# First adaptive modulation of a two-block network in three portions of its weights, and the order of work around three row norms

## The chip, the cores and the metric

One NeuronCore of one Trainium2 chip runs the whole program. The metric is the device time of one launch in microseconds (us), median over several runs; lower is better. A profiled execution of the same program gives the trace.

## The reference

Batch 1, 256 tokens `x` and 256 context tokens `ctx`, width 1024. A first network has two layers of adaptive normalisation: a retention mixer, then differential attention, each followed by a feed-forward network (FFN) with a convolution. A second network mixes two kinds of attention and a recurrence and ends in a plain FFN. All weights are float32. What the change touches first is the opening of layer 0:

```python
def ada_mod(cvec, w, b):                       # w: 1024 x 6144
    m = jax.nn.silu(cvec) @ w + b
    return jnp.split(m[:, None, :], 6, axis=-1)
shm, scm, gm, shf, scf, gf = ada_mod(c, ada_w[l], ada_b[l])
ux = modulate(rms_norm(h_x, norm_g[l, 0]), shm, scm)      # xn * (1 + scale) + shift
uc = modulate(rms_norm(h_c, norm_g[l, 0]), cshm, cscm)    # the same with c_ctx's vectors
p = u @ w_in                                              # first retention product, 1024 x 8192
```

Shift `shm` and scale `scm` are columns 0 to 2047 of `ada_w[0]` (8 MB). Feature f of 128 columns (f = 0 to 7) of the modulated rows needs only its own 128 columns of shift and of scale.

## The kernel before, in words

Every large product is done as three float32r products of high and low halves (`three`, L586). Weights come in steps of four units of 128 x 1024 (512 KB), one in each of four slots `raw[:, j]`. SyncE issues their loads in one fixed order (L465 to L571). For each unit ScalarE copies the high half to `wh` (L1548) and VectorE subtracts to get the low half `wl` (L2310); both functions are called `split`. TensorE then multiplies the unit (96 matmuls of 512 columns in a step of the retention input). A slot is reloaded once `lo_done` says that its low half is there. The order of work on each engine is written out by hand and semaphores join the engines; PSUM is used as two halves of four banks, `main` and `side`.

**The opening.** GpSimd issues the loads of the identity, the picks, the tokens (`load_residual`, L3344: 1 MB `x` into `res[:, 0:2]`, 1 MB `ctx` into `res[:, 2:4]`), then a dozen small vectors (`load_rows`, L3335), the bias table, and after `lo_done` reaches 2 (L3393) the two retention decays, the retention constants `kret` (1.1 MB) and a ring of later modulation weights (`load_mods`). SyncE loads columns 0 to 2047 of `ada_w[0]` in four chunks of 512 columns through the four `raw` slots (L502 to L508), a slot being loaded again when TensorE has used it (`ada_used`), and only then the first retention weights (`load`, L465). For chunk n TensorE multiplies the four units by the two condition vectors (`first_ada`, L744, matmuls at L633), ScalarE copies the result out (`keep_ada`, L1571), TensorE turns it (`turn_ada`, L637) and VectorE adds the bias (`take_ada`, L2351). ScalarE squares the token rows and takes roots (`row_square`, L1579), VectorE scales them (`normalise_row`, L2392), TensorE transposes two tiles of 128 tokens at a time into PSUM (`turn_part`, L731). When all four chunks are in, VectorE forms `1 + scale` times the gain (`scales`, L2403), and ScalarE (`apply_even`, L1587) and VectorE (`apply_part`, L2424) modulate feature by feature straight out of PSUM and write high and low halves `uh` and `ul`. The first retention step (L888) goes over its four units for tokens 0 to 255, takes the second pair of token tiles in between, and goes over the units again for the context. VectorE then computes the logarithm of the decays' sigmoid (`log_sigmoid`, L2490), and both engines wait for the constants before they split the second step's units (L1699, L1700, L2529).

**The three norms.** After differential attention (L1283), after the second FFN (L1293) and after the second network's mixer (L1520), 256 rows are normalised in two tiles. ScalarE takes the mean square of the product in PSUM (`rms`, L1617), VectorE scales and adds it to the residual (`finish_rows`, L2722), ScalarE squares the new residual (`norm_rows`, L1631), VectorE takes the reciprocal (L2453) and scales tile 0 (L2457), ScalarE scales tile 1 (L1639). In the second part ScalarE splits all four units of the next step (`split()`, L1870, L2259) before it waits for the new residual. TensorE transposes the tiles (`turn_normed`, L688) and fills its waits with matmuls of the identity (`keep_clock`, L720: 16 and 10 calls, two instructions each); `prep` (L1643, L2461) then modulates and forms halves, after which the next product starts. After the mixer there is no scaling between; VectorE adds the product to the residual (`add_plain`, L3272).

Of the kernel before, what the change touches and what calls it, by code (L numbers as in the profile page):

```python
# [8 lines left out]
ALU = mybir.AluOpType  # L9
# [174 lines left out]
def build(nc, a, out):  # L184
    ctx = ExitStack()
    with ctx:
# [76 lines left out]
        norm_a = (area(0, KD, SEQ), [area(8 + 4 * t, D) for t in range(4)])  # L263
# [107 lines left out]
        raw_loaded = [sem(f"raw_loaded{j}") for j in range(SLOTS)]  # L371
        hi_done = sem("hi_done")
# [32 lines left out]
        xn_act, xn_vec = sem("xn_act"), sem("xn_vec")  # L405
# [55 lines left out]
        def _(sp):  # L461
# [3 lines left out]
            def load(parts):  # L465

                s = S.next()
                for j in range(SLOTS):

                    if isinstance(s, int) and s == 0:  # L470
                        sp.wait_ge(ada_used, 12 + j + 1)
                    else:
                        sp.wait_ge(lo_done, s * SLOTS + (j - SLOTS + 1))
                    pieces = parts(j)
                    for dst, src in pieces:
                        sp.dma_start(dst, src).then_inc(raw_loaded[j], 32 // len(pieces))
# [33 lines left out]
            kq, kk, kv = RH * RDK, 2 * RH * RDK, RH * RDV  # L510
            for h in range(RH):
                load(pair(w, h * RDK, h * RDK + kq))
# [62 lines left out]
        def _(pe):  # L575
# [98 lines left out]
            def turn_rows(batch, n, loads):  # L674

                pe.wait_ge(rows_loaded[batch], 16 * loads)
                begin_row()
                pe.transpose(ps[:, main, 0:n], rows[0:n, batch, :], ident[0:n, 0:n]).then_inc(turned, 1)

            def begin_row():  # L680


                if G.next():
                    pe.wait_ge(emptied, G.now() - 1)
# [3 lines left out]
            def turn_normed(nt):  # L688
# [13 lines left out]
                for part in range(2):  # L702
                    for t in tiles_of(nt, part):
                        v, x = (vec_turned, act_turned)[t % 2], (xn_vec, xn_act)[t % 2]
                        v[0] += 1
                        pe.wait_ge(x, v[0])
# [11 lines left out]
            vec_turned, act_turned = [0], [0]  # L718
# [25 lines left out]
            def first_ada(n):  # L744

                if n > 1:
                    pe.wait_ge(ada_kept, n - 1)
                for u in range(SLOTS):
                    if (n, u) == (1, 2):
                        turn_part(0, norm_a[1][0:2], side)  # L750
                    pe.wait_ge(raw_loaded[u], 32 * (n + 1))
                    ada_matmuls(n, u, raw[:, u, :], main + 3 - n % 2)

            def first_turn(n):
# [3 lines left out]
                turn_ada(n, main + 1)  # L758

            first_ada(0)  # L760
            turn_rows(2, 96, 2)
            first_turn(0)
            first_ada(1)
            turn_rows(1, 113, 9)
            first_turn(1)
            first_ada(2)
            turn_rows(3, 88, 2)
            turn_rows(4, 88, 2)
            pe.wait_ge(hot_loaded, 32)
            pe.wait_ge(tab_set, 1)  # L770
            begin_row()
            pe.matmul(ps[0:16, main, 0:384], tab, hot, start=True, stop=True).then_inc(turned, 1)
            first_turn(2)
            first_ada(3)
            first_turn(3)

            def dense_tokens(half, passes=((0, 1, 2, 3),), fresh=0):
# [4 lines left out]
                for x, tiles in enumerate(passes):  # L782
                    for j in range(SLOTS):
                        pe.wait_ge(lo_done, base + j + 1)
                        if fresh:
                            pe.wait_ge(part_low, SLOTS * (fresh + x - 1) + j + 1)
                        for k in range(2):
                            f = 2 * j + k
                            for t in tiles:
                                mm = three(ps[:, half + t, :], uh[:, f, t * P:(t + 1) * P], ul[:, f, t * P:(t + 1) * P],  # L790
                                           wh[:, j, k * 512:(k + 1) * 512], wl[:, j, k * 512:(k + 1) * 512], f == 0, f == KD - 1)
                        if x == len(passes) - 1:
                            mm.then_inc(unit_used, 1)
                        yield SLOTS * x + j
# [87 lines left out]
            for h in range(RH):  # L882
                d = 4 * h
                dense = G.now()
                if h == 0:
                    pe.wait_ge(ada_kept, 4)
                    pe.wait_ge(ada_taken, 4)
                    for j in dense_tokens(main, ((0, 1), (2, 3)), fresh=1):  # L888
# [2569 lines left out]
```

## Time and profile before

| what | value |
|---|---|
| median of 3 runs | 1867.37 us (1866.85 to 1868.1) |
| the profiled execution, its own time | 1869.95 us |
| its span, first to last instruction | 1868.2 us |
| what lies around the span | 1.75 us |
| TensorE busy | 96% of the span |
| VectorE, ScalarE, GpSimd busy | 61%, 45%, 5% |
| mean granted TensorE clock | 0.986 of full speed |
| mean DMA rate | 151 GB/s |

TensorE's clock has two levels, 2.4 GHz (1.00) and 1.2 GHz (0.50). A busy share says how long instructions of an engine were in flight; adjacent matmuls overlap, so the distance between two starts is what one costs. Idle time matters only on the engine that everything else waits for.

### The profile page before, as it was taken

What the parts mean: (1) busy time and instruction counts of PE and PEld (TensorE: products, weight loads), DVE (VectorE), ACT (ScalarE), POOL (GpSimd) and SP (SyncE); (2) the same over time, 40 slices, a digit from 0 to 9 for tenths busy, and PEclk for the clock granted to TensorE, in tenths of its full rate; (3) what the DMA queues carried; (4) which work ended last, traced back from release to release, by engine and by line L of the source; (5) the groups of instructions that cost most, each with busy time, mean ns of one, the idle gap of its engine ahead of it and who ended that gap; (6) DMA issues with size and microseconds to landing.
All of it is one profiled execution on the core that took longest, in us unless ns stands there. A gap on an engine that the chain in (4) does not pass through costs nothing. (4 is left out here: it accounts for less than half of the span.)

```text
span 1868.2 us, 26242 instructions
## 1 busy us (share of the span) xinstructions
PE 1795.1 (96%) x9865; PEld 1499.7 (80%) x9865; DVE 1143.2 (61%) x1525; ACT 837.2 (45%) x1213; POOL 86.9 (5%) x164
## 2 busy tenths in 40 slices
PE   5999999999999999999998998899999999989997
PEld 2877777777678888888887887899879987879985
DVE  2766757667358678644347556566665695855554
ACT  3333233232456432233335556566554546544553
POOL 2011001100000010000000000000001000000000
PEclk8999999999999999999999999999999999999999
DMA  8654444545255376432323222455545554546562
GB/s 289 196 156 144 151 146 151 164 144 151 94 214 180 124 227 188 146 94 79 113 69 112 80 79 83 141 181 181 190 148 184 162 158 146 181 139 187 180 193 100
DMA packets 150909, 282.38 MB, mean 151 GB/s; under 512 B 12651, under 2 KB 78307, under 8 KB 150688
## 3 DMA queue, kind: packets, MB, share of 16 engines
q1 hardware_dynamic: 133344, 220.54, 36.9%
q0 software_dynamic: 17472, 60.57, 10.5%
q8 instruction: 63, 1.03, 0.2%
q14 instruction: 30, 0.25, 0.0%
HBM read 276.83 MB, written 4.23 MB: 150 GB/s over the span
## 5 line engine op out<-in xcount | busy, mean ns | idle before, releaser
L2310 DVE TENSOR_TENSOR wl<-raw,wh 128x1024 fp32r<-128x1024 f32 (+1 forms) x388 | 454.6, 1181 | 383.7 <-ACT wh L1548 381.3
L1548 ACT ACTIVATE wh<-raw 128x1024 fp32r<-128x1024 f32 (+1 forms) x388 | 393.5, 1022 | 617.5 <-PE ps L590 605.0
L588 PE MATMUL ps<-uh,wh 128*128 128x256 f32 (+1 forms) x1216 | 381.9, 314 | 7.8 <-DVE spare L2332 7.8
L589 PE MATMUL ps<-ul,wh 128*128 128x256 f32 (+1 forms) x1216 | 379.8, 312 | 0.0
L590 PE MATMUL ps<-uh,wl 128*128 128x256 f32 (+1 forms) x1216 | 379.6, 312 | 0.0
L588 PE MATMUL ps<-wh,uh 128*128 128x512 f32 (+2 forms) x960 | 367.4, 383 | 9.7 <-issue 6.2
L589 PE MATMUL ps<-wl,uh 128*128 128x512 f32 (+2 forms) x960 | 354.1, 369 | 0.0
L590 PE MATMUL ps<-wh,ul 128*128 128x512 f32 (+2 forms) x960 | 353.8, 369 | 0.0
L588 PEld LDWEIGHTS ps<-uh,wh 128*128 128x128 f32 x1216 | 233.9, 192 | 22.9 <-issue 7.0
L590 PEld LDWEIGHTS ps<-uh,wl 128*128 128x128 f32 x1216 | 233.8, 192 | 12.7
L589 PEld LDWEIGHTS ps<-ul,wh 128*128 128x128 f32 x1216 | 233.9, 192 | 12.3
L588 PE MATMUL ps<-wh,ah 128*128 128x512 f32 x584 | 229.3, 393 | 0.9 <-DVE al L2444 0.7
L590 PE MATMUL ps<-wh,al 128*128 128x512 f32 x584 | 227.4, 389 | 0.0
L589 PE MATMUL ps<-wl,ah 128*128 128x512 f32 x584 | 227.3, 389 | 0.0
L588 PEld LDWEIGHTS ps<-wh,uh 128*128 128x128 f32 x960 | 182.3, 190 | 52.8 <-issue 23.0
L589 PEld LDWEIGHTS ps<-wl,uh 128*128 128x128 f32 x960 | 182.4, 190 | 33.6 <-issue 5.3
L590 PEld LDWEIGHTS ps<-wh,ul 128*128 128x128 f32 x960 | 182.2, 190 | 30.7
L2371 DVE SCALAR_TENSOR_TENSOR arena<-arena,cvec 128x1024 f32<-128x1024 f32 x140 | 173.7, 1281 | 8.8 <-DMA arena<-in_ada_w 0.8
L588 PEld LDWEIGHTS ps<-wh,ah 128*128 128x128 f32 x584 | 109.6, 188 | 26.1 <-issue 3.4
L590 PEld LDWEIGHTS ps<-wh,al 128*128 128x128 f32 x584 | 109.6, 188 | 23.1
L589 PEld LDWEIGHTS ps<-wl,ah 128*128 128x128 f32 x584 | 109.7, 188 | 22.8 <-issue 0.5
L860 PE MATMUL ps<-res,arena 128*128 128x512 f32 x160 | 72.5, 600 | 3.0 <-DVE res L2607 2.1
(305 smaller groups left out, 1490.5 us busy)
## 6 DMA issues: line engine op xcount, KB each, us to landing
raw<-in_ffn_w_up SPq DMA_DIRECT2D x176, 256.0 KB
arena<-in_ada_w POOLq DMA_DIRECT2D x80, 512.0 KB, 4.1
raw<-in_w_in SPq DMA_DIRECT2D x60, 512.0 KB
raw<-in_ret_w_in SPq DMA_DIRECT2D x48, 512.0 KB
raw<-in_ffn_w_down SPq DMA_DIRECT2D x40, 512.0 KB
raw<-in_ret_w_out SPq DMA_DIRECT2D x32, 512.0 KB
raw<-in_w_up SPq DMA_DIRECT2D x32, 512.0 KB
raw<-in_w_down SPq DMA_DIRECT2D x32, 512.0 KB
```

The costliest lines, as they stand in the source:

```text
L588: pe.matmul(o, lh, rh, start=first, stop=False)
L589: pe.matmul(o, lh, rl, start=False, stop=False)
L590: return pe.matmul(o, ll, rh, start=False, stop=last)
L860: mm = pe.matmul(ps[:, half + t % 2, :], v0[:, c:c + P], vres[:, k, :], start=n == 0, stop=n == len(reads[t]) - 1)
L1548: T.mark(act.activation(wh[:, j, 0:size], raw[:, j, 0:size], ACT.Copy), hi_done)
L2310: T.mark(vec.tensor_tensor(wl[:, j, 0:size], raw[:, j, 0:size], wh[:, j, 0:size], ALU.subtract), lo_done)
L2371: ins = vec.scalar_tensor_tensor(out=o, in0=w, scalar=c32[:, k, c:c + 1], in1=o, op0=ALU.mult, op1=ALU.add)
```

## The change

1. **Portions.** The four chunks become: n = 0, columns 0 to 511 (shift of f = 0 to 3); n = 1, columns 1024 to 1535 (scale of f = 0 to 3); n = 2, shift and scale of f = 4, 5; n = 3, of f = 6, 7. Chunks 2 and 3 are loaded as two DMAs of 256 KB per unit (rows of 1 KB). So the first portion is chunks 0 and 1, the second chunk 2, the third chunk 3. Eight areas `first` of the arena hold them in place of the `raw` slots, so the first retention units can be loaded in between: units 0 and 1 after chunk 1, unit 2 after chunk 2, unit 3 after chunk 3.
2. **Tokens on SyncE's queue.** `x` and `ctx` are loaded by two DMAs of SyncE ahead of all weights. The later reload of the same two stays with GpSimd.
3. **Opening compute.** All four token tiles are transposed early; ScalarE and VectorE copy them to `xt` in SBUF and modulate from there (`apply_first`: on VectorE two scalings, the split of unit j, two subtractions). TensorE runs `keep_clock` with 20 calls, then multiplies the first retention step in one pass (`dense_first`, which waits before unit j for `lo_done` j + 1 and `part_low` 2j + 2), with chunks 2 and 3 and the small transposes between its eighths.
4. **Decays.** Their two small DMAs are issued before the wait, and `log_sigmoid` comes after the first portion. The constants' load waits for `ada_used` 16 in place of `lo_done` 2.
5. **Norms.** VectorE scales both tiles; ScalarE no longer waits for the reciprocal except for the one before; its splits go one unit per part (two after the mixer), the rest after the squares; VectorE's last two splits move into `prep`; `keep_clock` has 12 and 6 calls in place of 16 and 10.

```diff
+        rows_a, xt = [area(8 + 4 * t, D) for t in range(4)], area(24, KD, TOK)
+        first = [area(kb, UNIT) for kb in (0, 4, 40, 44, 54, 58, 71, 75)]
@@ sync
-            for c in range(4):
-                part = cols(a["ada_w"][0], c * 512)
-                for j in range(SLOTS):
-                    if c:
-                        sp.wait_ge(ada_used, 4 * (c - 1) + j + 1)
-                    for dst, src in part(j):
-                        sp.dma_start(dst, src).then_inc(raw_loaded[j], 32)
+            sp.dma_start(res[:, 0:2, :], a["x"][0].rearrange("(t p) n -> p t n", p=P)).then_inc(rows_in[0], 16)
+            sp.dma_start(res[:, 2:4, :], a["ctx"][0].rearrange("(t p) n -> p t n", p=P)).then_inc(rows_in[1], 16)
+            def load_first(n, u):
+                i = 4 * n + u
+                if i >= 8:
+                    sp.wait_ge(ada_used, i - 7)
...
+            for n in range(4):
+                for u in range(SLOTS):
+                    load_first(n, u)
+                for j in ((), (0, 1), (2,), (3,))[n]:
+                    load_unit(part, j)
@@ tensor
+            for u in range(2):
+                first_ada(0, u)
+            turn_part(0, rows_a[0:2], main)
+            for u in range(2, SLOTS):
+                first_ada(0, u)
+            pe.wait_ge(xt_act, 1)
+            pe.wait_ge(xt_vec, 1)
+            turn_part(2, rows_a[2:4], main)
             turn_rows(2, 96, 2)
+            for u in range(2):
+                first_ada(1, u)
+            turn_rows(1, 113, 9)
             first_turn(0)
+            for u in range(2, SLOTS):
+                first_ada(1, u)
             first_turn(1)
+            pe.wait_ge(xt_act, 2)
+            pe.wait_ge(xt_vec, 2)
+            keep_clock(ps[:, side + 3, 384:TOK], 20)
+            for j, k in dense_first(main):
+                if (j, k) in ((0, 0), (1, 0)):
+                    for u in range(SLOTS):
+                        first_ada(2 + j, u)
+                elif (j, k) in ((0, 1), (1, 1)):
+                    first_turn(2 + j)
+                    turn_rows(3 + j, 88, 2)
+                elif (j, k) == (2, 0):
+                    turn_table()
@@ turn_normed
-                                keep_clock(ps[:, halves[0] + 3, 384:TOK], 16)
+                                keep_clock(ps[:, halves[0] + 3, 384:TOK], 12)
-                        keep_clock(ps[:, halves[0] + 3, 384:TOK], 10)
+                        keep_clock(ps[:, halves[0] + 3, 384:TOK], 6)
@@ scalar, opening
+            def apply_first(j):
+                f = 2 * j
+                T.settle()
+                for k in range(2):
+                    x = xt[:, f, k * SEQ:(k + 1) * SEQ]
+                    T.mark(act.activation(x, x, ACT.Identity, scale=acol[:, k, f:f + 1], bias=mcols(k, f, 1)), act_own)
+                T.settle()
+                for k in range(2):
+                    act.wait_ge(part_odd, 2 * j + k + 1)
+                    T.mark(act.activation(uh[:, f:f + 2, k * SEQ:(k + 1) * SEQ], xt[:, f:f + 2, k * SEQ:(k + 1) * SEQ], ACT.Copy), part_hi)
+            squares(0)
+            squares(1)
+            keep_xt(0)
+            keep_ada(0, side + 3)
+            keep_xt(1)
+            keep_ada(1, side + 2)
+            split(units=range(0, 1))
+            act.wait_ge(acol_ready, norms[0])
+            apply_first(0)
+            split(units=range(1, 2))
+            apply_first(1)
             act.wait_ge(z_abs, 1)
             T.mark(act.activation(lgt[:, 2, :], lgt[:, 1, :], ACT.Exp, scale=-1.0), lg_exp)
+            for n in (2, 3):
+                keep_ada(n, side + 5 - n)
+                split(units=range(n, n + 1))
+                act.wait_ge(acol_ready, norms[0])
+                apply_first(n)
@@ scalar, norm_rows and finish_rows
+                if rms_parts[0] > 1:
+                    act.wait_ge(rstd_ready, rms_parts[0] - 1)
                 T.mark(rms(tiles, lambda t: res[:, t, :], D, (0, 4)), rms_done)
-                act.wait_ge(rstd_ready, rms_parts[0])
-                for t in tiles:
-                    if t % 2:
-                        T.mark(act.activation(xn[:, t, :], res[:, t, :], ACT.Copy, scale=st[:, 8 + t:9 + t]), xn_act)
...
-                    if part:
-                        split()
+                    split(units=range(part, part + 1))
                     wait_residual(part)
                     norm_rows(nt, part)
+                split(units=range(2, SLOTS))
@@ scalar, after the mixer
-                if part:
-                    split()
                 wait_residual(part)
                 norm_rows(2, part)
+                split(units=range(2 * part, 2 * part + 2))
@@ vector, opening
+            for t in range(3):
+                normalise_row(t, t, rows_a[t])
+            keep_xt(0)
+            normalise_row(3, 3, rows_a[3])
+            keep_xt(1)
             take_cols(bcol[:, :], 96)
             take_cols(gcol[:, 0:113], 113)
+            take_ada(0, side + 1)
+            take_ada(1, side + 1)
+            first_scales(0, 4)
+            apply_first(0)
+            apply_first(1)
+            log_sigmoid()
+            take_ada(2, side + 1)
+            first_scales(4, 6)
+            apply_first(2)
             take_cols(fcol2[:, :], 88)
             take_cols(fcol[:, 16:104], 88)
+            take_ada(3, side + 1)
+            first_scales(6, 8)
+            apply_first(3)
@@ vector, norm_rows and prep
-                    if t % 2 == 0:
-                        T.mark(vec.tensor_scalar(xn[:, t, :], res[:, t, :], st[:, 8 + t:9 + t], None, ALU.mult), xn_vec)
+                    T.mark(vec.tensor_scalar(xn[:, t, :], res[:, t, :], st[:, 8 + t:9 + t], None, ALU.mult), xn_vec)
...
+                    if half:
+                        split(units=range(2, 3))
                     hb = group_full()
...
+                split(units=range(3, 4))
@@ vector, finish_rows
-                    norm_rows(nt, part, range(2) if part else ())
-                split(units=range(2, SLOTS))
+                    norm_rows(nt, t, range(t, t + 1))
@@ gpsimd
-            load_residual()
...
+            for z, name in enumerate(("ret_decay_f", "ret_decay_b")):
+                pool.dma_start(lgt[:, 0, 4 * z:4 * z + 4], a[name].to_broadcast([P, RH])).then_inc(decay_loaded, 16)
...
-            pool.wait_ge(lo_done, 2)
-            for z, name in enumerate(("ret_decay_f", "ret_decay_b")):
-                pool.dma_start(lgt[:, 0, 4 * z:4 * z + 4], a[name].to_broadcast([P, RH])).then_inc(decay_loaded, 16)
+            pool.wait_ge(ada_used, 16)
```

## Rows read from the trace of the kernel before

**Rows 1.** the page, busy time of the engines over the whole span

```profile
PE 1795.1 (96%) x9865; PEld 1499.7 (80%) x9865; DVE 1143.2 (61%) x1525; ACT 837.2 (45%) x1213; POOL 86.9 (5%) x164
```

**Rows 2.** who TensorE waited for: total us, times, longest

```profile
PE ps L588 <- DVE spare L2332: 7.8, 3, 2.8
...
PE ps L699 <- DVE arena L2457: 5.6, 2, 4.2
```

**Rows 3.** stretches: length, busy time, TensorE clock, DMA share, GB/s

```profile
20.00:22.00 2.00, 2.00 (x15) 1.50 (x8) 0.00 (x0) 0.00 (x0) 0.00 (x0) 1.00 1.01 371
...
42.00:44.00 2.00, 0.12 (x1) 0.15 (x1) 1.97 (x3) 1.83 (x4) 0.00 (x0) 0.50 0.97 340
...
48.00:50.00 2.00, 2.00 (x7) 1.58 (x6) 1.97 (x3) 0.58 (x1) 0.83 (x2) 0.54 0.91 101
```

**Rows 4.** timeline of the opening: start us, us, engine, line, operation

```profile
12.26 1.06 ACT L1582 ACTIVATE junk<-res 128x1024 bf16<-128x1024 f32 x1 [6.39 <-DMA res<-in_x]
...
20.50 2.93 PE L737 MATMUL ps<-ident,arena 128*128 128x128 f32 x16
...
25.54 1.07 PE L633 MATMUL ps<-raw,cvec 128*32 128x256 f32 x16
...
39.38 0.98 PE L642 MATMUL ps<-pick,adas 128*128 128x4 f32 x4 [0.60 <-ACT adas L1577]
...
40.88 0.99 DVE L2415 TENSOR_SCALAR arena<-ps,acol,mcol 128x256 f32<-128x256 f32 x2
...
41.52 0.63 ACT L1598 ACTIVATE uh<-arena 128x512 fp32r<-128x512 f32 x1
...
41.80 1.21 DVE L2310 TENSOR_TENSOR wl<-raw,wh 128x1024 fp32r<-128x1024 f32 x1
...
43.04 0.69 DVE L2422 TENSOR_TENSOR ul<-arena,uh 128x512 fp32r<-128x512 f32 x1
...
43.88 0.77 PE L588 MATMUL ps<-wh,uh 128*128 128x512 f32 x1 [3.52 <-DVE ul L2422]
...
54.92 1.91 PE L737 MATMUL ps<-ident,arena 128*128 128x128 f32 x16
...
64.21 1.41 DVE L2504 SCALAR_TENSOR_TENSOR lgt<-lgt 128x12 f32<-128x12 f32 x7
...
70.54 1.03 ACT L1759 ACTIVATE arena<-ps 128x1024 f32<-128x1024 f32 x1 [1.27 <-PE ps L590]
```

**Rows 5.** DMA issues: size of one, us from issue to landing

```profile
arena<-in_k_ret POOLq DMA_DIRECT2D x1, 1152.0 KB, 8.7
```

**Rows 6.** timeline, first changed norm (after the second attention)

```profile
1186.10 5.37 PE L724 MATMUL ps<-ident 128*128 128x128 f32 x32
...
1187.72 1.23 DVE L2739 TENSOR_TENSOR res<-res,arena 128x1024 f32<-128x1024 f32 x1
...
1190.05 1.06 ACT L1624 ACTIVATE junk<-res 128x1024 bf16<-128x1024 f32 x1
...
1191.74 2.40 PE L724 MATMUL ps<-ident 128*128 128x128 f32 x20
...
1191.76 1.15 ACT L1639 ACTIVATE arena<-res,st 128x1024 f32<-128x1024 f32 x1 [0.23 <-DVE st L2453]
...
1193.97 1.04 PE L699 MATMUL ps<-ident,arena 128*128 128x128 f32 x8
...
1197.46 0.36 PE L588 MATMUL ps<-uh,wh 128*128 128x256 f32 x1 [2.45 <-DVE spare L2332]
```

**Rows 7.** timeline, second changed norm (after the second FFN)

```profile
1397.13 0.39 PE L588 MATMUL ps<-uh,wh 128*128 128x256 f32 x1 [2.57 <-DVE spare L2332]
```

**Rows 8.** timeline, third changed norm (after the mixer)

```profile
1663.75 1.22 DVE L3283 TENSOR_TENSOR res<-res,ps 128x1024 f32<-128x1024 f32 x1 [1.68 <-PE ps L590]
...
1667.79 1.06 ACT L1624 ACTIVATE junk<-res 128x1024 bf16<-128x1024 f32 x1
...
1674.56 0.55 PE L588 MATMUL ps<-uh,wh 128*128 128x256 f32 x1 [2.76 <-DVE spare L2332]
```

More of the change, by code:

```diff
@@ L371, in build @@
         raw_loaded = [sem(f"raw_loaded{j}") for j in range(SLOTS)]
+        first_loaded = [sem(f"first_loaded{j}") for j in range(8)]
+        xt_act, xt_vec = sem("xt_act"), sem("xt_vec")
+        rows_in = (sem("x_in"), sem("ctx_in"))
         hi_done = sem("hi_done")
@@ L468, in load, with load_unit @@
                 for j in range(SLOTS):
[L470 to L476, printed above, removed]
+                    sp.wait_ge(lo_done, s * SLOTS + (j - SLOTS + 1))
+                    load_unit(parts, j)
+            def load_unit(parts, j):
+                pieces = parts(j)
+                for dst, src in pieces:
+                    sp.dma_start(dst, src).then_inc(raw_loaded[j], 32 // len(pieces))
             def cols(w, c0, n=512):
@@ L677, in turn_rows @@
                 begin_row()
-                pe.transpose(ps[:, main, 0:n], rows[0:n, batch, :], ident[0:n, 0:n]).then_inc(turned, 1)
+                pe.transpose(ps[:, side, 0:n], rows[0:n, batch, :], ident[0:n, 0:n]).then_inc(turned, 1)
+            row_groups = Count()
             def begin_row():
-                if G.next():
-                    pe.wait_ge(emptied, G.now() - 1)
+                G.next()
+                if row_groups.next():
+                    pe.wait_ge(emptied, row_groups.now() - 1)
             turned_norms = [0]
@@ L757, in first_turn, with turn_table, dense_first @@
                     pe.wait_ge(ada_taken, n)
-                turn_ada(n, main + 1)
-            first_ada(0)
+                turn_ada(n, side + 1)
+            def turn_table():
+                pe.wait_ge(hot_loaded, 32)
+                pe.wait_ge(tab_set, 1)
+                begin_row()
+                pe.matmul(ps[0:16, side, 0:384], tab, hot, start=True, stop=True).then_inc(turned, 1)
+            def dense_first(half):
+                G.next()
+                S.next()
+                for j in range(SLOTS):
+                    pe.wait_ge(lo_done, j + 1)
+                    pe.wait_ge(part_low, 2 * j + 2)
+                    for k in range(2):
+                        f = 2 * j + k
+                        for t in range(4):
+                            mm = three(ps[:, half + t, :], uh[:, f, t * P:(t + 1) * P], ul[:, f, t * P:(t + 1) * P],
+                                       wh[:, j, k * 512:(k + 1) * 512], wl[:, j, k * 512:(k + 1) * 512], f == 0, f == KD - 1)
+                        if k:
+                            mm.then_inc(unit_used, 1)
+                        yield j, k
@@ L765, in _ @@
             first_turn(1)
[L766 to L777, printed above, removed]
+            pe.wait_ge(xt_act, 2)
@@ new lines, in apply_first @@
+            def apply_first(j):
+                f = 2 * j
+                for k in range(2):
+                    x = xt[:, f + 1, k * SEQ:(k + 1) * SEQ]
+                    T.mark(vec.tensor_scalar(x, x, acol[:, k, f + 1:f + 2], mcols(k, f + 1, 1), ALU.mult, ALU.add), part_odd)
+                split(units=range(j, j + 1))
+                T.settle()
+                for k in range(2):
+                    vec.wait_ge(part_hi, 2 * j + k + 1)
+                    o = slice(k * SEQ, (k + 1) * SEQ)
+                    T.mark(vec.tensor_tensor(ul[:, f:f + 2, o], xt[:, f:f + 2, o], uh[:, f:f + 2, o], ALU.subtract), part_low)
@@ L2520, in _ @@
             tick(emptied)
-            take_ada(2, main + 1)
-            for t in range(2, 4):
-                normalise_row(t, t, norm_a[1][t])
-            take_ada(3, main + 1)
-            scales(0, 8)
-            apply_part(0, side, norm_a[0], 0, 0, lambda j: split(units=range(j, j + 1)))
-            apply_part(1, side, norm_a[0], 1, 0)
-            log_sigmoid()
             vec.wait_ge(const_loaded, 16)
@@ L3292, in _ @@
                 norm_rows(2, part, range(2) if part else ())
-            split(units=range(2, SLOTS))
             prep(2, MLPG0, None)
```

151 lines of the change are left out of this document (74 added, 77 removed).

## The prediction

> **What bounds the kernel now.** First the page: TensorE has something in flight for 96% of the span, 1795.1 us, VectorE 61%, ScalarE 45% [rows 1]. So time is won only where TensorE waits or works at half rate. Then who it waited for: three times 2.6 us on average for the first half of a modulated norm, twice for normalised rows [rows 2]. The largest loss is the opening. In the timeline the first product that counts, a matmul of the retention step, starts at 43.88 us, released by the first feature's low half [rows 4]; what TensorE does before is small (condition vectors, transposes). From there it is not idle until long after, so whatever moves 43.88 forward moves the end, provided later inputs keep up. ScalarE's read of the first step's result at 70.54 marks where that step ends [rows 4].
>
> The clock needs care. The stretch from 20 to 22 us is printed with 1.00, yet 16 transposes started at 20.50 took 2.93 us, and the same 16 at 54.92 took 1.91 [rows 3, 4]; so part of the early work ran at 1.2 GHz although the column says otherwise. In 42 to 44 it is 0.50, and in 48 to 50 it is 0.54, which puts the rise at about 49.8 (0.5 and 1.00 weighted by time) [rows 3]. The step therefore spent 6.0 us at half rate, worth 3.0, then 70.4 - 49.8 - 1.9 for the transposes = 18.7: 21.7 us at full rate, 2.7 for an eighth of it.
>
> **Part 1, when the first portion is there.** Bytes move at 371 GB/s with rows of 2 KB or more, and at 340 with rows of 1 KB, both at full DMA share [rows 3]. Before the end of chunk 1 come 2.1 MB of tokens, 4.2 MB of chunks 0 and 1, and some 0.3 MB of small loads: 6.6 MB / 0.371 = 17.8 us, after about 3.3 us until the first bytes: 21.1. The tokens have to come anyway; ahead of the weights they delay chunk 0, and the squares can start near 7.5 instead of 12.26 [rows 4]. Each 512 KB unit of 1 KB rows then takes 1.54: units 0 and 1 by 24.2, chunk 2 by 30.4, unit 2 by 31.9, chunk 3 by 38.1, unit 3 by 39.6. SyncE's waits (`ada_used`, then `lo_done`) are all met by then. I count the 16 half-size DMAs and their issue at nothing beyond that rate, since the queue is ahead of the engines; if it weren't, the price is the second rival's.
>
> **Part 2, TensorE until the first product.** Chunk 0's first two units at about 12 to 14, the first transposes (16, up to 3.6 us if all at half rate, twice the 1.91 of full rate less overlap), chunk 0's rest to 19.5, the second transposes some 2.5 to 22. Then, at full rate: a turned bias 0.4, two units 1.07 (25.54 in [rows 4]), a wait of 0.3 for VectorE's copies, gains 0.4, turn 0.6, two units 1.07 to 25.9, ScalarE's copy 0.4, the second turn 0.6 to 27.0. That is 6 us behind the data, since the order on TensorE puts all four tiles first. VectorE adds and scales by 27.5. Then the 40 instructions of `keep_clock`: 20 took 2.40 us at full rate [rows 6], so 4.7, to 31.7.
>
> **Part 3, the first feature pair.** Unknown is modulation out of SBUF; from PSUM two of VectorE took 0.99, at 40.88 in [rows 4]. Nothing excludes a gain: between 0.4 and 1.0 for two. I take 0.8. Then VectorE's split 1.21 and two subtractions of 0.69 [rows 4]: with gaps 3.6 us. ScalarE's two modulations and two copies of 0.63 fit beside it. 27.5 + 3.6 = 31.1, so `keep_clock` covers this chain: the first product starts at 31.7, against 43.88. Between ends: 27.5 if the turns hurry and `keep_clock` does not bind, 36.4 if all of its 40 run at half rate (another 4.7).
>
> **Part 4, the first step with its guests.** Eight eighths 21.7; chunks 2 and 3, 32 instructions each at full rate, 2.1 each (two units 1.07) = 4.3; two turns (0.98 at half rate, 39.38 in [rows 4]) 1.2; three small transposes 1.7; waits between them 0.4: 29.3 us, to 61.0. The order waits for nobody: chunk 2 is there at 30.4 and wanted at 34.4; chunk 3 is there at 38.1 and wanted at 43. Unit 1's features are low at 34.5, wanted at 40. `log_sigmoid` (seven steps 1.41, some 4 in all [rows 4]) now stands on VectorE before `take_ada` 2: 34.5 to 38.6, while TensorE turns chunk 2 at 39.5, so it is covered by 1 us, and without cover costs at most 4 once. The third portion is turned at 48.5, plus 4.5 for scales and features = 53, wanted at 55. So the first step ends at 61.0 instead of 70.4: **9.4 us**. The transposes (1.9) that stood inside the step are in Part 2.
>
> The decays' DMAs are earlier and cost GpSimd two issues in a stretch in which nobody waits for it: nothing. The constants are issued at about 45 and land 8.7 later [rows 5], 54; a split on ScalarE (1.06) and VectorE (1.21) makes unit 0 of step 2 at 56.5, wanted at 61.
>
> **Part 5, the three norms.** In the first, ScalarE spent 3.9 us on four splits, so the squares of tile 1 came at 1190.05 though the residual was added at 1188.95; ScalarE's scaling ended at 1192.9, and TensorE, held by its own fillers (5.37 + 2.40), transposed at 1193.97 [rows 6]. Now: squares at 1189.0, root at 1190.5, VectorE's scaling (at most the 1.15 of ScalarE's, I take 0.8) ends 1191.5 instead of 1192.9. Fillers: 24 and 12 instructions in place of 32 and 20. Part of the first batch is at half rate (32 in 5.37 are 15 slow and 17 fast, at 0.23 and 0.117), so 24 are 4.5 and 12 are 1.4: transposes at 1192.4. Gain 1.6. ScalarE's last two splits end at 1192.7, in time; the split that VectorE now does between the halves (1.2) delays only units 2 and 3, which TensorE wants 5.8 us after it starts. The second has the same order, and there the last splits on ScalarE bind by 1.6 as well: its product would start near 1395.5 instead of 1397.13 [rows 7]. In the third the residual was ready at 1664.97 and the squares came at 1667.79, 2.8 late [rows 8]. Now squares at 1665.0, but VectorE does two splits (2.4) before the reciprocal, scaling done 1668.3, fillers (2.8 + 0.5 + 1.4 at full rate) until 1668.7, product at 1671.7 for 1674.56: 2.9. Together **6.1**. Between ends: 3 if the shorter fillers bring half-rate spells (each about 1.7, three of them would take 5.1; one is there already at the third), 8 if a spell disappears.
>
> Sum: 9.4 + 6.1 = 15.5 us. The profiled execution, 1869.95 with 1.75 around its span, would be 1854.4. The median of the runs is 2.6 below it: 1851.9, which I give as **1852**.
>
> **A rule against it.** TensorE's early transposes took 2.93 for 16 and by the time of 25.54 two units took 1.07, full rate, so the rise followed a burst of transposes [rows 4]. The Trainium skill, TensorE: Matmul & The Clock Gate, "PE-mode transpose", says that transposes do not count as TensorE being busy; the trace neither proves nor refutes it, as matmuls lay between. By the page the sum would be that of the first rival below; by the row it stays. This change puts 32 transposes where the clock would have to rise.
>
> **Rivals.**
> 1. *The clock rises late* (15%): `keep_clock` runs at half rate for most of its 40 (+3 to 4.7) and the first eighth too (+2.7 at most). For it: 0.50 up to 49.8 before. Against it: TensorE is busier from 14 us on. Time 1852 + 3 to 7, say 1857.
> 2. *A later portion comes late* (10%): if 1 KB rows move nearer to 290 GB/s, chunk 3 is there at 42 and unit 3 at 44; the half-size DMAs might add to it. TensorE has it on its own queue in front of ready eighths, so each us late after 43 is lost: 1 to 4, some 1855.
> 3. *The step's gain is handed back at step 2* (4%): constants land late because they share the queue with four units and two ring loads; if unit 0 of step 2 is ready only at 68 instead of 56.5, 7 of 9.4 are gone: 1859. The 4.5 us between 56.5 and 61 speak against it.
> 4. *Slower* (3%): the guests in the first step keep TensorE at 1.2 GHz through all of it. Then `keep_clock` costs 4.7 more, the eighths 21.7, the guests 4: 30 us against 15.5 won: 1882. It decides once about 15.5 us of full-rate work, from the start of `keep_clock` at 27, take twice their time, that is if the rise comes after 58. Before it came 6 us after the step began.
>
> **Numbers.** Forecast 68%, with its own range 1847 to 1856. Range for 8 in 10: from 1846 (first product at 28, or a spell less) to 1859 (rivals 1 to 3). A measurement tells 0.2%, 3.7 us, from no change. Faster by more: the forecast, rivals 1 and 2, and most of 3, less the tails: 93%. Within: 4%. Slower: 3%.
>
> **What would show it.** First matmul of the retention step at 31.7 released by its own queue or by the low half, not by a DMA; ScalarE's first PSUM read of step 1 at 61; no wait for chunks 2 and 3; 20 identity matmuls in 4.7 us; the three norms' products 1.6, 1.6 and 2.9 us nearer to the last matmul before them. Wrong if the first product starts after 36, if TensorE waits for DMA inside the step, if the clock column is 0.50 beyond 40, or if VectorE's split releases step 2's first matmul.

## The result, and the profile after

| | before | after |
|---|---|---|
| median of 4 runs, us | 1867.73 (1866.85 to 1868.12) | 1851.4 (1850.31 to 1854.96) |
| profiled execution, its span | 1869.95, 1868.2 | 1851.7, 1849.9 |

The ratio is 0.9918, with an interval of 0.9907 to 0.993: faster by 16.3 us in the medians and by 18.3 in the two spans. The forecast was 1852.

The page of the kernel after, its first lines and then TensorE's waits (us in total, times, longest one), against [rows 1, 2]:

```profile
span 1849.9 us, 26229 instructions
PE 1786.4 (97%) x9857; PEld 1495.8 (81%) x9857; DVE 1147.1 (62%) x1534; ACT 835.9 (45%) x1213; POOL 86.4 (5%) x162
...
PE ps L610 <- DVE spare L2406: 7.0, 3, 2.5
PE ps L655 <- DMA arena<-in_ada_w: 6.5, 2, 6.3
PE ps L724 <- DVE arena L2531: 6.3, 3, 4.2
```

The three waits for the first half of a modulated norm are hardly shorter (7.0 for 7.8). What was won there lies ahead of them, in the fillers and in the wait for them. The wait for modulation weights is now one of 6.3 us before the first chunk and one of 0.3 behind its first units; within the step there is none.

**The opening.** The timeline of the kernel after (start, duration, engine, line, operation, idle time before and its releaser in brackets):

```profile
7.75 1.06 ACT L1630 ACTIVATE junk<-res 128x1024 bf16<-128x1024 f32 x1
...
11.88 1.08 PE L655 MATMUL ps<-arena,cvec 128*32 128x256 f32 x8 [6.26 <-DMA arena<-in_ada_w]
...
14.24 3.68 PE L761 MATMUL ps<-ident,arena 128*128 128x128 f32 x16
...
19.28 1.94 PE L761 MATMUL ps<-ident,arena 128*128 128x128 f32 x16 [0.29 <-ACT arena L1736]
...
25.27 0.58 PE L664 MATMUL ps<-pick,adas 128*128 128x4 f32 x4 [0.59 <-ACT adas L1625]
...
25.71 4.71 PE L748 MATMUL ps<-ident 128*128 128x128 f32 x40
...
26.37 0.73 DVE L2608 TENSOR_SCALAR arena<-arena,acol,mcol 128x256 f32<-128x256 f32 x2
...
28.27 1.29 DVE L2614 TENSOR_TENSOR ul<-arena,uh 128x512 fp32r<-128x512 f32 x2
...
30.18 0.48 PE L610 MATMUL ps<-wh,uh 128*128 128x512 f32 x1
...
58.53 1.03 ACT L1834 ACTIVATE arena<-ps 128x1024 f32<-128x1024 f32 x1 [4.38 <-PE ps L612]
```

The first product stands at 30.18 instead of 43.88 [rows 4], with no wait ahead of it: its low half was ready at 29.56 (28.27 + 1.29) and the fillers ended at 30.4. ScalarE's first read of the step moved from 70.54 to 58.53. That is 12.0 us, two thirds of the 18.3. The first 16 transposes took 3.68 and the second 1.94: the clock rose between them, at about 18.

Stretches of the kernel after (busy time and instructions of PE, PEld, DVE, ACT, POOL, then the granted clock, the DMA share and GB/s):

```profile
16.00:18.00 2.00, 2.00 (x13) 1.67 (x16) 0.05 (x1) 0.05 (x1) 0.00 (x0) 1.00 1.02 192
28.00:30.00 2.00, 2.00 (x20) 2.00 (x19) 1.97 (x5) 1.97 (x4) 0.00 (x0) 1.00 1.09 379
34.00:36.00 2.00, 2.00 (x25) 1.24 (x18) 1.66 (x11) 0.91 (x2) 0.00 (x0) 1.00 1.09 384
...
1182.00:1184.00 2.00, 2.00 (x12) 2.00 (x11) 1.96 (x4) 0.58 (x2) 0.00 (x0) 0.50 0.09 18
```

In 28 to 36 the weights come in rows of 1 KB at 379 to 385 GB/s (the stretches between the two shown have 379 and 385), not at the 340 of [rows 3]. The fourth row is the price of the norm before it and is read below.

**The norms.** TensorE's timeline of the kernel after, first norm, then the first transpose and the first product of the two others:

```profile
1171.07 0.63 PE L724 MATMUL ps<-ident,arena 128*128 128x128 f32 x4 [4.16 <-DVE arena L2531]
1171.54 4.47 PE L748 MATMUL ps<-ident 128*128 128x128 f32 x24
...
1177.62 1.04 PE L724 MATMUL ps<-ident,arena 128*128 128x128 f32 x8
1181.11 0.36 PE L610 MATMUL ps<-uh,wh 128*128 128x256 f32 x1 [2.45 <-DVE spare L2406]
...
1371.25 0.63 PE L724 MATMUL ps<-ident,arena 128*128 128x128 f32 x4 [1.46 <-DVE arena L2531]
...
1380.31 0.58 PE L610 MATMUL ps<-uh,wh 128*128 128x256 f32 x1 [2.23 <-DVE spare L2406]
...
1648.16 0.60 PE L724 MATMUL ps<-ident,arena 128*128 128x128 f32 x4
...
1656.35 0.47 PE L610 MATMUL ps<-uh,wh 128*128 128x256 f32 x1 [2.27 <-DVE spare L2406]
```

The first transposes of the kernel before (its three products are in [rows 6, 7, 8]), and the stretch behind its first product:

```profile
1185.63 0.63 PE L699 MATMUL ps<-ident,arena 128*128 128x128 f32 x4 [4.15 <-DVE arena L2457]
...
1386.13 0.63 PE L699 MATMUL ps<-ident,arena 128*128 128x128 f32 x4 [1.46 <-DVE arena L2457]
...
1663.55 0.60 PE L699 MATMUL ps<-ident,arena 128*128 128x128 f32 x4
...
1198.00:1200.00 2.00, 2.00 (x19) 2.00 (x18) 1.94 (x5) 1.70 (x3) 0.00 (x0) 1.00 0.27 94
```

From the first transpose to the first product the three norms took 11.83, 11.00 and 11.01 us before and take 10.04, 9.06 and 8.19 now: 1.79, 1.94 and 2.82, together 6.5. But in 1182 to 1184, right behind the first norm's product, the clock is 0.50, where before it was 1.00. (Behind the products of the second and the third norm it falls in both kernels.) Such a stretch is 3.4 us long here and costs up to 1.7. Counted against the same instruction before (a split of weights on VectorE, which TensorE paces, or the norm's first transpose), the kernel after is ahead by 12.0 us at the end of the opening, 14.6 before the first norm, 14.9 behind it, 17.0 behind the second, 15.4 before the third and 18.2 behind it. So the first norm gave 0.3 of its 1.79, and a half-rate stretch at 1625.5, which before had not, took most of 1.7 back.

**A piece of the shift that the change did not make.** Between 600 and 630 the shift grew from 11.8 to 14.4. A stretch of the kernel before, then the one that answers to it of the kernel after, each with the wait of TensorE ahead of it:

```profile
618.49 1.06 PE L737 MATMUL ps<-ident,arena 128*128 128x128 f32 x8 [1.71 <-DVE arena L2397]
...
620.00:622.00 2.00, 2.00 (x10) 2.00 (x11) 0.02 (x1) 0.09 (x1) 0.00 (x0) 0.50 0.00 0
```

```profile
605.62 1.06 PE L761 MATMUL ps<-ident,arena 128*128 128x128 f32 x8 [0.63 <-DVE arena L2472]
...
608.00:610.00 2.00, 2.00 (x19) 2.00 (x18) 1.38 (x3) 1.65 (x3) 0.00 (x0) 1.00 0.03 8
```

1.1 us less wait for normalised rows and a half-rate stretch less make the 2.6. No line of the change acts there, and experiment 2 shows that the change is not needed for it. There the opening is that of the kernel before and nothing is altered ahead of the first norm, yet the same place looks as in the kernel after:

```profile
616.41 1.07 PE L736 MATMUL ps<-ident,arena 128*128 128x128 f32 x8 [0.62 <-DVE arena L2393]
...
620.00:622.00 2.00, 2.00 (x19) 2.00 (x19) 1.59 (x4) 1.94 (x5) 0.00 (x0) 1.00 0.00 0
```

Of all the profiles only two have the longer wait and the half-rate stretch here: the one of the kernel before, and that of experiment 7 (a wait of 2.2 us, the stretch at 609.6); a third, `fill_transposes`, has a wait of 1.8 and no stretch. So the 2.6 belongs to the single profiled execution of the kernel before, which lay 2.2 us above its median. Why TensorE comes late to that wait in some executions was not traced.

### The profile page after: what moved, and what is told of

The parts are those of the page before. It is cut to its first block and busy times, and to the rows that moved or that the text cites. A ratio compares the mean times of both kernels' runs of the same rounds, so it can differ in the third digit from the quotient of the medians.

```text
span 1849.9 us, 26229 instructions
## 1 busy us (share of the span) xinstructions
PE 1786.4 (97%) x9857; PEld 1495.8 (81%) x9857; DVE 1147.1 (62%) x1534; ACT 835.9 (45%) x1213; POOL 86.4 (5%) x162
## 3 DMA queue, kind: packets, MB, share of 16 engines
q0 software_dynamic: 16928, 58.47, 10.2%
## 5 line engine op out<-in xcount | busy, mean ns | idle before, releaser
L612 PEld LDWEIGHTS ps<-uh,wl 128*128 128x128 f32 x1216 | 234.1, 193 | 12.5
L612 PEld LDWEIGHTS ps<-wh,ul 128*128 128x128 f32 x960 | 181.7, 189 | 30.4
```

Source lines behind the costliest of these rows:

```text
L612: return pe.matmul(o, ll, rh, start=False, stop=last)
```

## The experiments

Each is the kernel after with one edit, except `norms_only`. "Step end" is ScalarE's first read of step 1 (58.53 after, 70.54 before); "intervals" are the three norms' as above. The kernel before ran beside each: 1868.19 for experiments 1 to 4, 1867.97 for 5, 6, 7 and `fill_transposes`, 1866.96 for `transposes_twice`, 9 and 10. The kernel after gave 1851.4 once and 1853.35 in experiment 10, so medians less than 2 us apart say nothing by themselves; there the step's end and the intervals are read. What the expectations call a spell is a stretch at half rate.

**1. The opening alone**, with the norms as before (`opening_only`, the diff's part 5 undone).

> The changed kernel with the three norms as they were before; only the opening is changed. Theory A (the two parts add up, and one more half-rate spell of the clock eats part of the norms' gain): the opening alone is worth the 12.35 us by which all later splits stand earlier, so 1867.7 - 12.3 = 1855.4, up to 1.7 less or more with a spell. Rival B (the norms' gain is lost wholly, all of the 16.3 us are the opening's): 1851.4. Rival C (the norms do most of it): above 1860.

1855.73 (1855.21 to 1857.9), ratio 0.9933 [0.9919, 0.9946]: 12.5 us. Step end 57.75, intervals 11.83, 11.01, 11.01. The 12.35 us of the expectation was read too high: the traces of before and after are 12.0 apart behind the opening, and the forecast of 1855.4 would have been 1855.7.

**2. The norms alone** (`norms_only`, the kernel before with part 5).

> The kernel before with only the norms' part of the change. Theory A: the three intervals from the first transpose to the first product shorten by 1.8, 1.9 and 2.8 us as in the changed kernel, 6.5 in all, less at most one spell of 1.7: 1861 to 1863. Rival B: 1867.7, no change, each interval's gain returned as a half-rate spell of 3.4 us behind it (1.7 each). Rival C: 1857 or less.

1863.17 (1860.87 to 1865.03), 0.9974 [0.9964, 0.9984]: 5.0 us. Intervals 10.12, 9.06, 8.20, so 6.5 won, of which the median shows 5.0 (its interval reaches from 3.0 to 6.7). In the profile the kernel is 4.1 us ahead already before the first norm, where its code is that of the kernel before (2.6 of it is the place at 620), and 8.0 behind the third: 3.9 across the norms. Half-rate stretches stand behind the first product, where before had none, and around the start of the second for 6.8 us, where before had 3.4. The two parts add up to 17.5 where both together gave 16.3, within what the runs scatter.

**3. The norms' fillers at their old length, in the new order** (`norm_fill_16_10`).

```diff
-                                keep_clock(ps[:, halves[0] + 3, 384:TOK], 12)
+                                keep_clock(ps[:, halves[0] + 3, 384:TOK], 16)
-                        keep_clock(ps[:, halves[0] + 3, 384:TOK], 6)
+                        keep_clock(ps[:, halves[0] + 3, 384:TOK], 10)
```

> The changed kernel with the norms' identity matmuls back at 16 and 10 calls; the new order of squares, splits and scalings stays. Theory A (TensorE's own fillers were the last thing the transposes waited for in the first and third norm, the splits in the second): the first and third norm give back 1.8 and about 2, the second 1: 1851.4 + 4 to 5 = 1856, unless the longer fillers save a spell (then 1854). Rival D (the order on ScalarE and VectorE made all the gain): 1851.4.

1853.51 (1849.49 to 1855.15), 0.9921 [0.9907, 0.9935]. Intervals 11.82, 9.82, 9.98: of the 6.5 us, 4.3 hang on the shorter fillers (1.8, 0.8 and 1.8); the new order alone gives nothing in the first norm, 1.2 in the second and 1.0 in the third. Yet the median is only some 2 above that of the kernel after. In its profile there is no half-rate stretch behind the first and the third product; behind the second there still is one, from about 1380.7. TensorE's row of the first product, and the stretch behind it:

```profile
1180.77 0.36 PE L610 MATMUL ps<-uh,wh 128*128 128x256 f32 x1 [2.45 <-DVE spare L2406]
...
1182.00:1184.00 2.00, 2.00 (x19) 2.00 (x18) 1.91 (x5) 0.65 (x2) 0.00 (x0) 1.00 0.18 40
```

The wait is the same 2.45 as in the kernel after, where 0.50 followed. Over all profiles the first norm sorts by its fillers: with 16 and 10 calls (before, experiments 1 and 3) none of three has a half-rate stretch behind the product, with 12 and 6 (in two of them as transposes) and the gap left open all nine have one. So the wait alone does not decide; that it is the amount of idle time around it is the likely reading, but no run varies that by itself.

**4. Fillers where TensorE is idle last**, between the last transposes and the product (`fill_before_product`).

```diff
                         keep_clock(ps[:, halves[0] + 3, 384:TOK], 6)
+                keep_clock(ps[:, halves[0] + 3, 384:TOK], 10)
```

> The changed kernel with 10 more calls (20 matmuls of the identity, 2.4 us at full rate) behind the last transposes of each of the three norms, in the 2.2 to 2.5 us in which TensorE waits there for the first product's inputs. Theory E (that idle time is what brings the half-rate spell of 3.4 us right behind the first product, seen at 1181.8, 1379.7 and 1656.2 in the changed kernel): the three spells go, 1851.4 - 3 x 1.7 = 1846.3. Rival F (the spell comes from elsewhere, or the fillers run late and hold up the product): 1851.4 to 1853.

1847.39 (1845.47 to 1851.1), 0.9892 [0.9877, 0.9908]: faster than both kernels, by 4.0 than the kernel after (against 1851.4, which ran at another time; `tuned` of experiment 10, with the same fillers, is 5.6 below the kernel after beside it). The intervals are unchanged to 0.01 us, and no half-rate stretch stands behind the three products:

```profile
1175.96 1.04 PE L724 MATMUL ps<-ident,arena 128*128 128x128 f32 x8
1176.83 2.40 PE L749 MATMUL ps<-ident 128*128 128x128 f32 x20
1179.45 0.36 PE L610 MATMUL ps<-uh,wh 128*128 128x256 f32 x1 [0.22 <-DVE spare L2407]
...
1180.00:1182.00 2.00, 2.00 (x19) 2.00 (x18) 1.96 (x4) 0.60 (x1) 0.00 (x0) 1.00 0.05 8
```

**5. All portions before the first product** (`one_portion`): chunks 2 and 3 are multiplied and turned first.

```diff
+            for j in range(2):
+                for u in range(SLOTS):
+                    first_ada(2 + j, u)
+                first_turn(2 + j)
+                turn_rows(3 + j, 88, 2)
+            turn_table()
             for j, k in dense_first(main):
-                if (j, k) in ((0, 0), (1, 0)):
...
+                pass
```

> The changed kernel, but TensorE multiplies and turns chunks 2 and 3 and all small transposes before the first eighth of the retention step, which then runs undivided; loads, tokens and all else as changed. Theory A (the data of chunk 3 are there near 38.5, so the step starts near 41 to 42 instead of 30.15 but then needs 21.8 instead of 28.4 us): it ends at 63 to 64 instead of 58.5, so 1851.4 + 5 = 1856.5, up to 1859 if the waits cost clock. Rival H (the portions are nearly all of the opening's gain): 1861 or more. Rival I (the earlier loads alone do it, the portions nothing): 1851.4.

1861.42 (1859.93 to 1864.46), 0.9966 [0.9954, 0.9978]. The size was missed: the step ends at 67.31, 8.8 us later, not 5, and the median is where the expectation's rival H had put it (1861 or more). The timeline and two stretches show why:

```profile
35.62 0.64 PE L655 MATMUL ps<-arena,cvec 128*32 128x256 f32 x8 [0.61 <-DMA arena<-in_ada_w]
37.02 1.08 PE L655 MATMUL ps<-arena,cvec 128*32 128x256 f32 x8 [0.76 <-DMA arena<-in_ada_w]
...
43.26 0.79 PE L610 MATMUL ps<-wh,uh 128*128 128x512 f32 x1
...
36.00:38.00 2.00, 1.24 (x16) 0.20 (x8) 1.94 (x5) 1.68 (x4) 0.00 (x0) 0.76 1.09 386
46.00:48.00 2.00, 2.00 (x8) 1.57 (x7) 0.04 (x1) 0.00 (x0) 0.00 (x0) 0.68 1.00 401
...
67.31 1.03 ACT L1833 ACTIVATE arena<-ps 128x1024 f32<-128x1024 f32 x1 [4.38 <-PE ps L612]
```

TensorE waits for unit after unit, and the same eight matmuls take 0.64 at 35.62 and 1.08 at 37.02: from 37.0 to 47.3 the clock is at half rate, well into the product, which is worth up to 5.1 of the 8.8. So the portions earn twice: the product starts 13 us earlier, and the long product keeps TensorE busy while the rest of the weights land.

**6. Tokens on GpSimd's queue** (`tokens_pool`): the two loads of `x` and `ctx` stand behind the picks, as before the change.

```diff
-            sp.dma_start(res[:, 0:2, :], ...).then_inc(rows_in[0], 16)
-            sp.dma_start(res[:, 2:4, :], ...).then_inc(rows_in[1], 16)
             pool.dma_start(picks[:, :], a["k_pick"]).then_inc(pick_loaded, 16)
+            pool.dma_start(res[:, 0:2, :], ...).then_inc(rows_in[0], 16)
+            pool.dma_start(res[:, 2:4, :], ...).then_inc(rows_in[1], 16)
```

> The changed kernel with the two token loads back on GpSimd's queue, where they stood. Theory A (the tokens share the DMA engines with the weights and land near 12 and 16 instead of 7.7 and 10.7; the small vectors wait behind them; TensorE's fixed order passes this on): first product 2 to 3 us later, 1854. Rival J (the bytes are the same and the portion's data land at the same time, so the queue doesn't matter): 1851.4.

1854.06 (1851.71 to 1854.61), 0.9917 [0.9904, 0.9931]; step end 59.50. TensorE's weight load now waits 7.8 us in 3 waits for normalised rows, and the one of 6.6 is in the opening:

```profile
PEld ps L759 <- DVE arena L2470: 7.8, 3, 6.6
```

The step's end comes 1.0 later, half or less of what was expected. In the runs the two kernels' intervals overlap; the size of about 1 us rests on the step's end alone.

**7. No fillers in the opening** (`no_open_fill`).

```diff
-            keep_clock(ps[:, side + 3, 384:TOK], 20)
```

> The changed kernel without the 20 calls (40 matmuls of the identity, 4.7 us) before the first product. The low half of the first features is there 0.6 us before that product starts. Theory K (the fillers hold the clock; 3.7 us of idle TensorE bring one or two half-rate spells, 1.7 each): product 0.5 earlier, end 1 to 3 us later, 1853. Rival L (the clock holds without them): 1850.9.

1855.07 (1853.27 to 1856.35), 0.9926 [0.9913, 0.994].

```profile
29.45 0.76 PE L610 MATMUL ps<-wh,uh 128*128 128x512 f32 x1 [4.12 <-DVE ul L2613]
...
26.00:28.00 2.00, 0.00 (x0) 0.00 (x0) 1.72 (x3) 1.88 (x5) 0.00 (x0) 0.53 1.06 367
28.00:30.00 2.00, 0.56 (x1) 0.50 (x2) 1.99 (x5) 1.97 (x4) 0.00 (x0) 0.50 1.09 384
30.00:32.00 2.00, 2.00 (x6) 1.60 (x5) 1.82 (x3) 1.95 (x5) 0.00 (x0) 0.50 1.09 384
```

The product starts 0.73 earlier and the step ends 0.96 later (59.49): 1.7 us lost to the clock, where the fillers cost 0.7. The median is 3.7 above 1851.4; the half-rate stretch at 609.6 in this profile shows that part of that has nothing to do with the opening.

**8. Transposes as fillers, half as long** (`fill_transposes`) **and equally long** (`transposes_twice`).

```diff
-                for _ in range(n):
-                    pe.matmul(o, ident[:, :], ident[:, :], start=True, stop=True)
+                for _ in range(2 * n):            # range(n) in fill_transposes
+                    pe.transpose(o, ident[:, :], ident[:, :])
```

> The changed kernel with every filler a transpose of the identity instead of a matmul of it, same number, shape and place (20 calls in the opening, 12 and 6 in each norm). Rival M (the Trainium skill, TensorE: Matmul & The Clock Gate, PE-mode transpose: transposes do not count as TensorE being busy): the clock falls or stays at half rate behind the fillers, so each of the four places starts its product with a longer spell, 1 to 4 us each: 1855 or more. Theory N (they count as matmuls do here): 1851.4, within 1.5.

> Every filler is two transposes of the identity in place of one matmul of it, which is two instructions; so instruction count and time of the fillers are those of the changed kernel (40, 24 and 12), which the single transposes weren't. Rival M (transposes do not count as activity): the clock falls during the opening's fillers as it did without them, so first product at half rate, step end 1 us later or more, and the norms' products too: 1854 or more. Theory N (they count as matmuls do): no spell in the opening, first product at 30.2, 1851.5.

`fill_transposes`: 1852.27 (1849.25 to 1856.16), 0.9913 [0.9899, 0.9926]. A transpose is one instruction, an identity matmul two, so the fillers were only 2.38 us long and 1.90 idle followed; a half-rate stretch at 29.0 has two possible causes, and the run tells them not apart. `transposes_twice` was sent for that: 1853.08 (1851.07 to 1855.25), 0.992 [0.9906, 0.9934], where the kernel after, repeated beside it, gave 1853.35.

```profile
26.08 7.50 PE L748 MATMUL ps<-ident 128*128 128x128 f32 x40
33.34 0.47 PE L610 MATMUL ps<-wh,uh 128*128 128x512 f32 x1
...
28.00:30.00 2.00, 2.00 (x12) 2.00 (x11) 1.97 (x4) 1.97 (x4) 0.00 (x0) 0.50 1.08 377
30.00:32.00 2.00, 2.00 (x11) 2.00 (x10) 1.87 (x4) 1.97 (x4) 0.00 (x0) 0.50 1.09 378
32.00:34.00 2.00, 2.00 (x17) 1.92 (x16) 1.57 (x5) 1.76 (x3) 0.00 (x0) 0.97 1.09 384
```

The clock fell at 25.5, just before the fillers began, and the 40 took 7.50 instead of 4.71; the step ended at 61.73, 3.2 late. But it rose again at about 32, while nothing had run on TensorE for six microseconds but transposes, and in the norms the same edit gave intervals of 9.99, 9.06 and 8.11. So in this run the clock rose while only transposes ran, and in the kernel after, too, its rise at about 18 came at the end of 16 transposes that took 3.68 us. Why it fell at 25.5, ahead of the first filler, stays open; the waits there (0.60 before the turn) are those of the kernel after.

**9. The decays' logarithm late** (`late_sigmoid`): the call and ScalarE's exponential stand behind the last portion again.

```diff
             apply_first(1)
-            log_sigmoid()
             take_ada(2, side + 1)
...
             tick(emptied)
+            log_sigmoid()
             vec.wait_ge(const_loaded, 16)
```

> The changed kernel with the logarithm of the decays' sigmoid, and its exponential on ScalarE, behind the last portion instead of behind the first. Theory (nobody waits for it in either place, its 4 us are covered): no change, 1851.4, step end at 58.5. Rival: the second step's units, whose split waits for it on ScalarE, come late and TensorE waits 1 to 4 us at 58.5: 1853 to 1855.

1852.15 (1849.86 to 1854.09), 0.9924 [0.991, 0.9937]: no difference; the step ended at 57.61, with no wait of TensorE from 28 to 75.

**10. The kernel after again, and a version with the fillers set anew** (`after_again`, `tuned`): the fillers of experiment 4, the second filler of a norm 3 calls instead of 6, the opening's 17 instead of 20.

> The changed kernel itself, unaltered, for a comparison on one chip with the next three. All theories: 1851 to 1852.5.

> The changed kernel with the 10 calls of fillers behind the last transposes of each norm, 17 calls in the opening in place of 20, and 3 in place of 6 as the norms' second batch. Theory E (idle time ahead of a product brings the spell behind it): the spells behind the three products are absent, 4 to 5 us below the unaltered kernel, and about 1 us more from the shorter fillers: 1846. Rival F (the earlier gain of such fillers was chance in where spells fall): 1851.

`after_again` 1853.35 (1850.37 to 1854.36), 0.9919 [0.9906, 0.9933]. `tuned` 1847.74 (1846.86 to 1849.07), 0.9896 [0.988, 0.9911]: 5.6 less. The intervals are 10.20, 9.06 and 8.10 beside 10.93, 9.06 and 8.20, the step ends at 57.45 for 58.29, and no half-rate stretch stands behind the products. Against experiment 4 nothing is settled: the ratios overlap, and the further microsecond that was expected was not seen.

## Why the prediction was right

**Part 1, the data: right, with one rate too low.** Squares started at 7.75 (7.5 foreseen), and no portion was waited for inside the step. The rows of 1 KB moved at 379 to 385 GB/s where I took 340 from [rows 3].

The Trainium skill, DMA: Bandwidth & Descriptors, "Measured (HBM→SBUF, 128 partitions, SWDGE, issued from GpSimd)", advises DMAs of at least 1 MiB for three quarters of the peak. SyncE's 256 KB ones ran here at 379 to 385 GB/s, against 371 for those of 512 KB in [rows 3], so the trace does not show that loss on this queue.

**Parts 2 and 3, the first product: 1.5 us too late.** The second turn ended at 25.85 (27.0 foreseen), as the data were not what bound it. VectorE's two modulations out of SBUF took 0.73 (0.8 taken), the chain 3.2 (3.6), the fillers 4.71 (4.7): they bound, as said, by 0.6.

**Part 4, the first step: 28.35 us against 29.3.** The step ended at 58.53 against 61.0, so 9.4 became 12.0. This is the mis-sized term: 1.5 ahead of the product and 0.95 within the step. `log_sigmoid`, the decays and the constants cost nothing, as put; the constants landed in 5.5 us rather than 8.7.

**Part 5, the norms: 6.5 against 6.1 in the intervals (1.79, 1.94, 2.82 for 1.6, 1.6, 2.9), but 5.0 in the time** when they were changed alone. The lower bound, that shorter fillers bring half-rate stretches of up to 1.7 each, is what happened once: behind the first norm's product. I had the mechanism as a bound and did not take it into the sum. Experiments 4 and 10 show what the three such stretches behind products cost the kernel after together: 4.0 us by the one; by the other 5.6, which includes shorter fillers. Two of the three stretches were in the kernel before as well.

**What lay outside the sum.** By the profiles the sum was 15.5 and the shift 18.3: 2.6 more in the opening, 2.6 at 620, 0.4 more in the intervals, less 1.5 behind the first norm's product and 1.6 at 1625.5; that makes 18.0, and the rest is in pieces of 0.3 and less. By the medians it was 15.5 against 16.3. The profiled execution of before lay 2.2 above its median, that of after 0.3, which is the difference; the 2.6 at 620 is most of the first. So that 1852 met 1851.4 within 0.6 is in part luck: an opening that was put 2.6 too small is set against two half-rate stretches that were not in the sum, stretches of that size come and go between executions of one program, and its runs spread from 1850.31 to 1854.96.

**The rivals.** The first (the clock rises late) did not happen: from about 18 on the opening ran at full rate. (In the kernel before, the rise fell inside the 16 transposes of [rows 4], whose 2.93 us lies between 3.68 at half and 1.91 at full rate; the prediction has matmuls between the two.) Its mechanism is real, though: experiments 5, 7 and 8 show it at 10.2, 6.8 and 6.8 us of half rate in the same place, the last with the step's end 3.2 late, which is the size I gave it. The rule of the Trainium skill, TensorE: Matmul & The Clock Gate, "PE-mode transpose", that transposes don't count as TensorE being busy, did not decide this case, and experiment 8 speaks against it: the clock rose at about 32 with only transposes running. That it fell just before them stays open. The second (a portion late) did not: the rate was 377 GB/s and more, and no wait stands inside the step. The third (constants late) did not happen either: no wait of TensorE from 30.18 to 75. The fourth would have needed a rise after 58; it came at 18.

## What to carry to other kernels

- Where a first product waits for a modulation, cut the weights by the features that it needs first: it starts early, and its own length then covers the rest of the loads and keeps the clock up. Both count; here the first step ended 8.8 us later without the portions, up to 5.1 of it by the clock.
- Fillers belong into the last idle stretch before a long product, not only between the steps ahead of it. When an interval is shortened, look at the clock of the 4 us behind it: that is where it is given back.
- A gain in an interval on TensorE is a gain in time only when the stretch behind runs at the same clock; compare shifts of the same instruction far behind it.

## What the runs showed of the hardware that was not expected

- The clock's column says 1.00 for the opening's first microseconds although instructions show half rate: 16 transposes took 3.68 us in a stretch whose rows, as 16 to 18 above, print 1.00, and 1.94 from 19.28 on. In these traces durations have to be used until the first change that it shows.
- A wait of 2.2 to 2.5 us before a product was followed by half rate in the kernel after, and a like one of 2.45 was not in the first norm of experiment 3, where 8 and 8 more filler instructions ran ahead of it. Fillers of 2.40 in the gap itself removed it in all three places, in experiment 4 and again in `tuned`.
- The same program differs from profile to profile in its half-rate stretches: the kernel after had seven between 900 and 1700 us, one of them of 6.8 us, its repetition seven with two of 6.8, and the first norm's interval was 10.04 in one and 10.93 in the other. The kernel before has a half-rate stretch and a longer wait at 620, together 2.6 us, that its own code does not show in experiment 2. One pair of profiles can be off by that much.
- Loads of 256 KB in rows of 1 KB moved at 377 to 385 GB/s from 24 to 38 us in the kernel after.
